# A two-layer encoder: expert weights loaded in 4 KB rows, tokens and results passed through DRAM in slot order

## The chip, the cores and the metric

The kernel runs on one core of a Trainium2 chip. The metric is the device time of one execution in microseconds. Engines are named as in the profile: PE is TensorE (PEld its weight loads), DVE is VectorE, ACT is ScalarE, POOL is GpSimd, SP is SyncE, which here issues the weight loads.

## The reference, cut to what matters

256 tokens of width 1024 pass two layers. Each has a mixer of three branches and a feed-forward part; the second layer's feed-forward part is a mixture of 8 experts of inner width 3584, of which each token takes two:

```python
def swiglu(h, w1, w3, w2):
    return (jax.nn.silu(h @ w1) * (h @ w3)) @ w2

def moe_ffn(h, router, w1, w3, w2):
    logits = (h @ router).astype(jnp.float32)
    top_v, top_i = lax.top_k(logits, TOP_K)
    top_w = jax.nn.softmax(top_v, axis=-1)
    gates = jnp.sum(jax.nn.one_hot(top_i, N_EXPERTS, dtype=jnp.float32) * top_w[..., None], axis=-2)
    ...
    y = gates[..., 0:1] * swiglu(h, w1[0], w3[0], w2[0])
    for e in range(1, N_EXPERTS):
        y = y + gates[..., e:e + 1] * swiglu(h, w1[e], w3[e], w2[e])
    return y
```

All data are float32. The last layer's output is normalized and multiplied by `g_final`.

## The kernel before

**Precision.** A float32 product is made of three products of float32r halves: `mm3` multiplies high by high, high by low and low by high. So each weight tile of 1 MB (a **unit**, 128 partitions x 2048) passes three steps: ACT copies it to its high half `ehi` (`unit_hi`, L830), DVE subtracts to get the low half `elo` in the place of the raw tile (`unit_lo`, L1232), and PE takes 12 matmuls of 512 columns with it (L1397 to L1399).

**Slots.** In the expert stage the tokens of an expert sit in a slot of 128 rows; an expert with more than 128 tokens would get an extra slot of its own. With these inputs there are 8 slots, 0 to 7. Slot 0 is written out, the others are a loop over `s` on each engine (`slot(s)`). A slot has 42 units: per step `f` of 512 inner columns two units each of w1, w3 and w2 (`expert_step`), w2 one step behind the others.

**The path through a slot.** PE writes h@w1 to PSUM `big[0]` and h@w3 to `big[1]`. ACT takes the SiLU into `hid` (L853), DVE multiplies (L1354), PE turns the block with four transposes (L1442; positions `HIDDEN`), ACT and DVE evict it as high and low half (`eahi` L860, `ealo` L1369; positions `TURNED`), and the w2 units use it. After the slot's last unit ACT evicts the result to `ysb` (L841).

**One-hot products.** The tokens of a slot are picked by matrix products: DVE builds the one-hot matrix `Gm` of the next slot, and `gather` (L1718) multiplies `xn` by it in two groups of eight float32 matmuls (16 rows in the trace), after units 38 and 39. Results go back by `spread` (L1727): four float32 matmuls of 512 columns with the turned gate matrix `GT`, after units 4, 6, 8 and 10 of the next slot, each added to `X` by DVE. `GT` is made by two transposes after unit 17. The last slot is spread behind the loop (L1808).

**Buffers.** SP loads units into a ring of 14 (`RING`): the load of unit n waits for PE to be done with unit n-14. `ehi` has three buffers (`EHI`), so ACT's copy of unit n waits for `eunit_done` of unit n-3. Engines run their programs in the order written and meet in semaphores alone; nothing reorders them. GpSimd does little: small loads, and one multiply of `xn` by `g_ffn` (L598) before the stage.

Of the kernel before, what the change touches and what calls it, by code (L numbers as in the profile page):

```python
# [50 lines left out]
FC = 512  # L51
STEPS = FE // FC
UNITS = 6 * STEPS
RING, EHI = 14, 3
# [89 lines left out]
def encoder(nc, ins, out):  # L144
    ctx = ExitStack()
    with ctx:
# [22 lines left out]
        X = keep("X", [P, NB, D])  # L169
        xn = keep("xn", [P, NB, D])  # L170
# [3 lines left out]
        tab = keep("tab", [P, T_W])  # L174
        bmask = keep("bmask", [P, HEADS, SCORE])
        mmask = keep("mmask", [P, SCORE])
        pcol = keep("pcol", [P, ROWS])
# [34 lines left out]
        sd = w("sd", o, [P, 2 * HEADS, SCORE])  # L212
        bhi[2], blo[2] = w("chi", o, [P, 4, TOKENS], F32R), w("clo", o + 4096, [P, 4, TOKENS], F32R)
# [50 lines left out]
        ehi = [w(f"ehi{i}", 8192 * i, [P, 4, 512], F32R) for i in range(EHI)]  # L264
# [3 lines left out]
        at_unit += [8192 * (EHI + i) for i in range(RING - E_GATES - E_MERGED)]  # L268
        assert at_unit[-1] + 8192 <= o
        eraw = [w(f"eraw{i}", a, [P, 4, 512]) for i, a in enumerate(at_unit)]  # L270
        elo = [w(f"elo{i}", a, [P, 4, 512], F32R) for i, a in enumerate(at_unit)]
# [7 lines left out]

        hid = [at(f"hid{i}", over_h + 2048 * i, [SLOT, FC]) for i in range(2)]  # L280
        ahi = [at(f"eahi{i}", over_h + 4096 + 2048 * i, [P, 4, SLOT], F32R) for i in range(2)]
        alo = [at(f"ealo{i}", over_h + 8192 + 2048 * i, [P, 4, SLOT], F32R) for i in range(2)]
        ysb = at("ysb", over_h + 12288, [SLOT, D])
# [25 lines left out]
        gfin = keep("gfin", [P, D])  # L309
        gffn = keep("gffn", [P, D])  # L310

# [88 lines left out]
        g_ready = sem("g_ready")  # L400
        gg_ready = sem("gg_ready")
# [16 lines left out]
        skew_row = HEADS * (2 * TOKENS - 1)  # L418

# [46 lines left out]
        def expert_step(n):  # L466


            if n < 4:
                return 0, n // 2, n % 2  # L470
            if n >= UNITS - 2:
                return STEPS - 1, 2, n % 2
            f, m = (n - 4) // 6 + 1, (n - 4) % 6
            return (f, m // 2, m % 2) if m < 4 else (f - 1, 2, m % 2)


        HIDDEN = [6 * f + 3 if f else 5 for f in range(STEPS)]
        TURNED = [min(6 * f + 5, UNITS - 2) if f else 7 for f in range(STEPS)]
        W1_END = [6 * f - 1 if f else 1 for f in range(STEPS)]
        W3_END = [6 * f + 1 if f else 3 for f in range(STEPS)]  # L480

# [25 lines left out]
        def _(sp):  # L507
# [12 lines left out]
            def expert_unit(e, n):  # L520

                f, m, j = expert_step(n)
                if m < 2:
                    src = ins[("moe_w1", "moe_w3")[m]][0, bass.ds(e, 1), 512 * j:512 * j + 512, FC * f:FC * f + FC]
                else:
                    src = ins["moe_w2"][0, bass.ds(e, 1), FC * f:FC * f + FC, 512 * j:512 * j + 512]
                return src.rearrange("e (k p) n -> p (e k) n", p=P)

            def load_expert(s, e, first=False):
                for n in range(UNITS):  # L530
# [12 lines left out]
                    sp.dma_start(eraw[n % RING][:, :, :], expert_unit(e, n)).then_inc(eraw_in[n % RING], 16)  # L543
# [14 lines left out]
        def _(pool):  # L558
# [27 lines left out]

            pool.wait_ge(x_ready, 8)
# [13 lines left out]


# [4 lines left out]
        EARLY = EHI  # L607
        def gather_bank(s, i):

            return 2 if isinstance(s, int) and s == 0 and i == 1 else 3  # L610
# [6 lines left out]
        def _(act):  # L617
# [219 lines left out]

            def outputs(s):
# [3 lines left out]

            def slot(s, first=False):
                for n in range(UNITS):
                    if not first or n >= EARLY:
# [15 lines left out]
                gathered(s + 1, 1)
# [1003 lines left out]
```

## Time and profile before

| | |
|---|---|
| median of 3 runs | 1719.37 us (1718.28 to 1719.67) |
| the profiled execution | 1720.06 us, of which its span 1718.2 us |
| expert stage, from PE's first unit | about 700 us to 1705 us of the span |
| PE busy | 1676.8 us, 98% |
| weights moved in the expert stage | 336 loads of 1024 KB |

A matmul's end is modelled in the profile, so that neighbours overlap; the time that one takes from its engine is the distance between the starts of two in a row. Where the timeline merges a row (x4), its start is that of the first.

### The profile page before, as it was taken

Reading aid. Unit: us, or ns where it says so; the run is one execution under the profiler, and the core shown is the slowest. Engines: PE = TensorE matmul, PEld = TensorE weight load, DVE = VectorE, ACT = ScalarE, POOL = GpSimd, SP = SyncE. Lnnn points to the kernel's source line nnn. Section 1 sums busy time; section 2 is a strip of 40 time slices with the busy share of each in tenths; the row PEclk is TensorE's granted clock in tenths of the full one; section 3 lists DMA queues with packets and bytes.
Section 4 is the critical chain, followed back from the end, with each engine's and each line's share of the span. In section 5 each row is a group of like instructions: output and inputs, shape, how many; then the busy total and the mean of one; then the engine's idle time right before and its main releaser. Section 6 shows DMA issues by size and latency. Waiting matters only on the chain.

```text
span 1718.2 us, 23329 instructions
## 1 busy us (share of the span) xinstructions
PE 1676.8 (98%) x9215; PEld 1434.6 (83%) x9215; DVE 1269.4 (74%) x991; ACT 1052.6 (61%) x950; POOL 18.7 (1%) x28
## 2 busy tenths in 40 slices
PE   5999999999999999999999999999999999999997
PEld 4899989999889997778788788788788788788786
DVE  4655665544566466898888888898898898888896
ACT  4365645443536454666776776676776777677675
POOL 1000000000000001000000000000000000000000
PEclk8999999999999999999999999999999999999999
DMA  7544454555654448999899999999999999999980
GB/s 236 194 142 145 147 195 148 194 178 176 206 178 142 147 148 318 343 348 376 316 349 374 328 365 354 327 371 344 336 374 339 341 370 338 345 370 339 344 296 25
DMA packets 234687, 468.54 MB, mean 273 GB/s; under 512 B 7553, under 2 KB 11745, under 8 KB 234625
## 3 DMA queue, kind: packets, MB, share of 16 engines
q1 hardware_dynamic: 232400, 459.17, 75.8%
q0 software_dynamic: 1936, 7.44, 1.3%
q8 instruction: 46, 0.75, 0.2%
q10 hardware_dynamic: 288, 1.05, 0.1%
q14 instruction: 17, 0.13, 0.0%
HBM read 465.53 MB, written 2.10 MB: 272 GB/s over the span
## 4 chain that ended last, share of the span: by engine, by line
PE 91%; DVE 4%; ACT 3%; DMA 1%; issue 1%; SPq 0%; DVEq 0%; ACTq 0%
PE big L1397 21%; PE big L1399 21%; PE big L1398 21%; PE small L1397 7%; PE small L1399 7%; PE small L1398 7%; PE small L1442 2%; DVE elo L1232 2%; PE small L1727 1%; ACT ehi L830 1%; PE small L1718 1%; DMA raw<-w_in 1%; ACT whi L628 1%; DVE wlo L906 0%; PE small L1557 0%
## 5 line engine op out<-in xcount | busy, mean ns | idle before, releaser
L1232 DVE TENSOR_TENSOR elo<-eraw,ehi 128x2048 fp32r<-128x2048 f32 x336 | 768.5, 2293 | 106.5 <-ACT ehi L830 105.2
L830 ACT ACTIVATE ehi<-eraw 128x2048 fp32r<-128x2048 f32 x336 | 643.2, 1918 | 180.7 <-PE big L1399 136.8
L906 DVE TENSOR_TENSOR wlo<-raw,whi 128x2048 fp32r<-128x2048 f32 (+2 forms) x104 | 229.9, 2218 | 200.7 <-ACT whi L628 200.7
L1397 PE MATMUL big<-ehi,hehi 128*128 128x512 f32 x896 | 363.6, 406 | 1.4 <-DVE helo L1277 1.4
L628 ACT ACTIVATE whi<-raw 128x2048 fp32r<-128x2048 f32 (+2 forms) x104 | 192.5, 1860 | 264.3 <-PE big L1399 203.5
L1399 PE MATMUL big<-ehi,helo 128*128 128x512 f32 x896 | 350.0, 391 | 0.0
L1398 PE MATMUL big<-elo,hehi 128*128 128x512 f32 x896 | 349.3, 390 | 0.0
L1397 PE MATMUL big<-hhi,whi 128*128 128x256 f32 x864 | 248.1, 287 | 9.8 <-DVE hlo L926 9.8
L1398 PE MATMUL big<-hlo,whi 128*128 128x256 f32 x864 | 245.9, 285 | 0.0
L1399 PE MATMUL big<-hhi,wlo 128*128 128x256 f32 x864 | 245.8, 284 | 0.0
L1397 PEld LDWEIGHTS big<-ehi,hehi 128*128 128x128 f32 x896 | 168.3, 188 | 40.9 <-issue 5.1
L1398 PEld LDWEIGHTS big<-elo,hehi 128*128 128x128 f32 x896 | 168.5, 188 | 38.1 <-issue 5.0
L1399 PEld LDWEIGHTS big<-ehi,helo 128*128 128x128 f32 x896 | 168.1, 188 | 36.4
L1397 PE MATMUL small<-ehi,eahi 128*128 128x512 f32 x448 | 179.8, 401 | 4.0 <-DVE elo L1232 4.0
L1397 PEld LDWEIGHTS big<-hhi,whi 128*128 128x128 f32 x864 | 167.2, 194 | 12.8 <-DVE hlo L926 10.7
L1399 PE MATMUL small<-ehi,ealo 128*128 128x512 f32 x448 | 174.8, 390 | 0.0
L1398 PE MATMUL small<-elo,eahi 128*128 128x512 f32 x448 | 174.6, 390 | 0.0
L1398 PEld LDWEIGHTS big<-hlo,whi 128*128 128x128 f32 x864 | 167.2, 193 | 0.6 <-issue 0.5
L1399 PEld LDWEIGHTS big<-hhi,wlo 128*128 128x128 f32 x864 | 167.2, 194 | 0.0
L1397 PEld LDWEIGHTS small<-ehi,eahi 128*128 128x128 f32 x448 | 84.2, 188 | 27.1 <-DVE elo L1232 6.3
L1398 PEld LDWEIGHTS small<-elo,eahi 128*128 128x128 f32 x448 | 84.2, 188 | 18.2 <-issue 1.7
L1399 PEld LDWEIGHTS small<-ehi,ealo 128*128 128x128 f32 x448 | 84.1, 188 | 17.8
(296 smaller groups left out, 1689.8 us busy)
## 6 DMA issues: line engine op xcount, KB each, us to landing
eraw<-moe_w SPq DMA_DIRECT2D x336, 1024.0 KB, 5.1
raw<-ffn_w SPq DMA_DIRECT2D x30, 1024.0 KB, 5.0
raw<-w_gate SPq DMA_DIRECT2D x24, 1024.0 KB, 5.0
raw<-w_in SPq DMA_DIRECT2D x20, 1024.0 KB, 5.0
raw<-w_branch SPq DMA_DIRECT2D x12, 1024.0 KB, 5.0
raw<-w_o SPq DMA_DIRECT2D x8, 1024.0 KB, 5.0
raw<-w_in SPq DMA_DIRECT2D x4, 896.0 KB, 4.8
raw<-ffn_w SPq DMA_DIRECT2D x6, 512.0 KB, 3.6
```

The costliest lines, as they stand in the source:

```text
L628: act.activation(whi[u % HI][:, 0:kt, 0:cols], raw[u % RAW][:, 0:kt, 0:cols], ACT.Copy).then_inc(hi_ready, 1)
L830: act.activation(ehi[n % EHI][:, :, :], eraw[n % RING][:, :, :], ACT.Copy).then_inc(ehi_ready, 1)
L906: dve.tensor_tensor(wlo[u % RAW][:, 0:kt, 0:cols], raw[u % RAW][:, 0:kt, 0:cols], whi[u % HI][:, 0:kt, 0:cols].bitcast(F32), ALU.subtract) ...
L1232: dve.tensor_tensor(elo[n % RING][:, :, :], eraw[n % RING][:, :, :], ehi[n % EHI][:, :, :].bitcast(F32), ALU.subtract).then_inc(elo_ready, 1)
L1397: pe.matmul(o, sh, mh, start=start, stop=False, **kw)
L1398: pe.matmul(o, sh, ml, start=False, stop=False, **kw)
L1399: return pe.matmul(o, sl, mh, start=False, stop=stop, **kw)
L1442: return pe.transpose(o, src, ident[0:n, 0:n])
L1718: m = pe.matmul(small[:, gather_bank(s, i), SLOT * k:SLOT * k + SLOT], xn[:, b, (4 * i + k) * P:(4 * i + k + 1) * P], Gm[:, b, :], start=b ...
L1727: pe.matmul(small[:, 3, :], GT[:, i // 2, :], ysb[:, half:half + 512], start=True, stop=True).then_inc(spread_done, 1)
```

## The change

**Units.** The inner columns are cut by 1024 (three blocks of 1024, one of 512: `PAIRS`, `pair_width`). A w1 or w3 unit is 256 weight rows of 1024 columns (4 KB in DRAM for each row in place of 2 KB; the last block keeps 512 columns), a w2 unit 256 rows of all 1024 columns. Still 42 units of 1 MB and 12 matmuls each, in the order of `ORDER`. With block p and matrix m (0, 1, 2 for w1, w3, w2) the units are 0-3 (0,0), 4-7 (0,1), 8-11 (1,0), 12-15 (1,1), 16-19 (0,2), 20-23 (2,0), 24-27 (2,1), 28-31 (1,2), 32-33 (3,0), 34-35 (3,1), 36-39 (2,2), 40-41 (3,2). SiLU and multiply take 1024 columns at once; hidden blocks are turned after the units in `TURNS`.

**High halves.** `ehi` has a fourth buffer. Units 0 to 35 go round four buffers, units 36 to 41 round three (`HI_OF`).

**Tokens and results.** GpSimd fills two DRAM tensors with zeros while the dense layer runs, scatters the tokens' rows into `xs_all` in slot order (four indirect transfers in slot 0), and loads a slot's rows for PE, which now turns them with two groups of four transposes, after units 35 and 36 (`GATHERS`). A slot's result is written to `y_all`. In slot 7, four indirect transfers fetch the rows that belong to the tokens, each followed by a multiply and an addition on GpSimd. The last slot is spread by product as before, its `GT` now made behind the loop.

```diff
-FC = 512
-STEPS = FE // FC
-UNITS = 6 * STEPS
-RING, EHI = 14, 3
+ORDER = [(p, m, q) for p, m in ((0, 0), (0, 1), (1, 0), (1, 1), (0, 2), (2, 0), (2, 1), (1, 2), (3, 0), (3, 1), (2, 2), (3, 2))
+         for q in range(pair_units(p))]
+UNITS = len(ORDER)
+TURNS = [9, 10, 18, 19, 30, 31, 37]
+GATHERS = [35, 36]
+RING, EHI, EHI_WORK = 14, 4, 3
+HI_OF = [n % 4 if n < 36 else (n - 36) % 3 for n in range(UNITS)]
...
-        ehi = [w(f"ehi{i}", 8192 * i, [P, 4, 512], F32R) for i in range(EHI)]
+        ehi = [w(f"ehi{i}", 8192 * i, [P, 2048], F32R) for i in range(EHI_WORK)]
+        ehi.append(at("ehi3", over_h, [P, 2048], F32R))
...
+                p, m, q = ORDER[n]
                 if m < 2:
-                    src = ins[("moe_w1", "moe_w3")[m]][0, bass.ds(e, 1), 512 * j:512 * j + 512, FC * f:FC * f + FC]
+                    rows = D // pair_units(p)
+                    src = ins[("moe_w1", "moe_w3")[m]][0, bass.ds(e, 1), rows * q:rows * q + rows,
+                                                       PAIR * p:PAIR * p + pair_width(p)]
-                    src = ins["moe_w2"][0, bass.ds(e, 1), FC * f:FC * f + FC, 512 * j:512 * j + 512]
+                    r = PAIR * p + 256 * q
+                    src = ins["moe_w2"][0, bass.ds(e, 1), r:r + 256, :]
...
+            pool.wait_ge(x_ready, 4)
+            pool.memset(zeros[:, :], 0.0).then_inc(zero_ready, 1)
+            pool.wait_ge(zero_ready, 1)
+            for s in range(SLOTS + 1):
+                pool.dma_start(xs_all[SLOT * s:SLOT * s + SLOT, :], zeros[:, :]).then_inc(zeroed, 16)
+            for s in range(NE - 1, SLOTS):
+                done = y_out if s == NE - 1 else zeroed
+                pool.dma_start(y_all[SLOT * s:SLOT * s + SLOT, :], zeros[:, :]).then_inc(done, 16)
...
+            pool.wait_ge(rows_ready, 1)
+            for c in range(2):
+                for b in range(NB):
+                    pool.indirect_dma_start(xs_all[:, :], bass.IndirectOffsetOnAxis(ap=rowi[:, c, b:b + 1], axis=0),
+                                            xn[:, b, :], None).then_inc(scattered, 16)
+            pool.wait_ge(scattered, 16 * 2 * NB)
+            def slot_in(s):
+                pool.dma_start(xs, xs_all[bass.ds(SLOT * s, SLOT), :]).then_inc(xs_in, 16)
...
+            with pool.Fori(1, last + 1) as s:
+                pool.wait_ge(marked, 2 * s - 1)
+                pool.wait_ge(he_ready, 2 * s + 2)
+                pool.tensor_tensor(mark[:, :], eps[:, :], eps[:, :], ALU.add).then_inc(marked, 1)
+                slot_in(s + 1)
+                pool.wait_ge(marked, 2 * s)
+                pool.wait_ge(y_ready, s)
+                pool.tensor_tensor(mark[:, :], eps[:, :], eps[:, :], ALU.add).then_inc(marked, 1)
+                pool.dma_start(y_all[bass.ds(SLOT * (s - 1), SLOT), :], ysb[:, :]).then_inc(y_out, 16)
+            pool.wait_ge(y_out, 16 * (last + 1))
+            for i in range(2 * NB):
+                pool.indirect_dma_start(ysb[:, :], None, y_all[:, :],
+                                        bass.IndirectOffsetOnAxis(ap=rowi[:, c, b:b + 1], axis=0)).then_inc(early_in, 16)
+                pool.wait_ge(early_in, 16 * (i + 1))
+                pool.tensor_scalar(ysb[:, :], ysb[:, :], gch[:, c, b:b + 1], None, ALU.mult).then_inc(early_scaled, 1)
+                pool.wait_ge(early_scaled, i + 1)
+                pool.tensor_tensor(X[:, b, :], X[:, b, :], ysb[:, :], ALU.add).then_inc(early_added, 1)
...
+                    act.wait_ge(eunit_done, UNITS * s + hi_before(n))
+                act.activation(ehi[HI_OF[n]][:, :], eraw[n % RING][:, :], ACT.Copy).then_inc(ehi_ready, 1)
...
+                        act.wait_ge(y_out, 16 * s)
                         outputs(s - 1)
+                    for p in range(PAIRS):
+                        if n == unit_end(p, 0) + 4:
+                            act.activation(hid[:, 0:pair_width(p)], flat2(big[0][0:SLOT, :, :])[:, 0:pair_width(p)],
+                                           ACT.Silu).then_inc(sil_done, 1)
+                    if n - 4 in GATHERS:
+                        gathered(s + 1, GATHERS.index(n - 4))
+                    if n - 4 in TURNS:
+                        turned(s, t)
...
+            act.wait_ge(early_added, 2 * NB)
             outputs(last)
...
+                if l:
+                    dve.wait_ge(zeroed, 16 * (SLOTS + 1 + SLOTS - NE))
+                    dve.wait_ge(y_out, 16)
...
                     if n == 19 and first:
+                        destinations()
+                    if n == 21 and first:
...
-                    if n == 20:
-                        picked(s + 1)
-                        gated(s + 1)
+                    for p in range(PAIRS):
+                        if n == unit_end(p, 1) + 3:
+                            dve.wait_ge(eunit_done, UNITS * s + unit_end(p, 1) + 1)
+                            dve.wait_ge(sil_done, PAIRS * s + p + 1)
+                            cols = slice(0, pair_width(p))
+                            dve.tensor_tensor(hid[:, cols], hid[:, cols], flat2(big[1][0:SLOT, :, :])[:, cols],
+                                              ALU.mult).then_inc(act_done, 1)
+                    if n - 4 in GATHERS:
+                        gathered(s + 1, GATHERS.index(n - 4))
+                    if n - 4 in TURNS:
+                        turned(s, TURNS.index(n - 4))
...
+            gated(last)
+            dve.wait_ge(gt_done, 1)
...
-            def spread(s, i):
-                pe.matmul(small[:, 3, :], GT[:, i // 2, :], ysb[:, half:half + 512],
-                          start=True, stop=True).then_inc(spread_done, 1)
...
+                    if m == 2:
+                        pe.wait_ge(alo_ready, HE * s + (HE if p == PAIRS - 1 else 2 * p + 1 + q // 2))
...
+                    i.then_inc(eunit_done, 1)
+                    if n in TURNS:
+                        t = TURNS.index(n)
+                        pe.wait_ge(act_done, PAIRS * s + t // 2 + 1)
+                        if t == HE - 1:
+                            pe.wait_ge(he_ready, 2 * s + 3)
                         for k in range(4):
+                            i = turn(small[:, turn_bank(t), SLOT * k:SLOT * k + SLOT], hid[:, c:c + P], SLOT)
+                        i.then_inc(hid_turned, 1)
+                    if n in GATHERS:
+                        j = GATHERS.index(n)
+                        if j == 0:
+                            pe.wait_ge(xs_in, 16 * (s + 1))
+                            pe.wait_ge(alo_ready, HE * s + HE - 1)
...
-                            pe.wait_ge(spread_added, 4 * s)
-                        i.then_inc(gt_done, 1)
-                    if n == UNITS - 4:
-                        pe.wait_ge(gt_ready, s + 1)
-                        gather(s + 1, 0)
-                    if n in HIDDEN:
+                            i = turn(small[:, gather_bank(j), SLOT * k:SLOT * k + SLOT], xs[:, (4 * j + k) * P:(4 * j + k + 1) * P])
...
```

**ACT, the end of a slot** (`REGISTER_ALU` rows carry the waits for the loads). Before, from unit 40's copy (`eraw_149`; unit 41's is `eraw_150`):

```order
L830 ACTIVATE ehi_135<-eraw_149 128x2048 [waits eunit_done]
L834 ISA
L835 ACTIVATE hehi<-small 128x512 [waits gather_done]
L859 REGISTER_ALU
L860 ACTIVATE eahi_172<-small 128x512 [waits hid_turned]
L829 REGISTER_ALU [waits eraw_in13]
L830 ACTIVATE ehi_136<-eraw_150 128x2048 [waits eunit_done]
L834 REGISTER_ALU
L835 ACTIVATE hehi<-small 128x512 [waits gather_done]
```

Now, from unit 39's copy (`eraw_150`) to behind unit 41's (`eraw_152`):

```order
L958 ACTIVATE ehi_135<-eraw_150 128x2048 [waits eunit_done]
L962 ISA
L963 ACTIVATE hehi<-small 128x512 [waits gather_done]
L957 REGISTER_ALU [waits eraw_in12]
L958 ACTIVATE ehi_136<-eraw_151 128x2048 [waits eunit_done]
L962 REGISTER_ALU
L963 ACTIVATE hehi<-small 128x512 [waits gather_done]
L957 REGISTER_ALU [waits eraw_in13]
L958 ACTIVATE ehi_137<-eraw_152 128x2048 [waits eunit_done]
L973 REGISTER_ALU
L975 ACTIVATE last_hi<-small 128x512 [waits hid_turned]
```

Each copy waits until the unit three back is finished, as before: 39's for unit 36, 41's for unit 38. The first gather is evicted behind 39's copy and not behind 40's, the last hidden block (`last_hi`) behind 41's and not ahead of it.

**DVE, the same place.** Before (`elo_163` is unit 40's):

```order
L1232 TENSOR_TENSOR elo_163<-eraw_149,ehi_135 128x2048 [waits ehi_ready]
L1276 ISA
L1277 TENSOR_TENSOR helo<-small,hehi 128x512 [waits hehi_ready]
L1369 TENSOR_TENSOR ealo_174<-small,eahi_172 128x512 [waits ahi_ready]
L1231 REGISTER_ALU
L1232 TENSOR_TENSOR elo_164<-eraw_150,ehi_136 128x2048 [waits ehi_ready]
L1276 REGISTER_ALU
L1277 TENSOR_TENSOR helo<-small,hehi 128x512 [waits hehi_ready]
```

Now (`elo_164` is unit 39's):

```order
L1378 TENSOR_TENSOR elo_164<-eraw_150,ehi_135 128x2048 [waits ehi_ready]
L1422 ISA
L1423 TENSOR_TENSOR helo<-small,hehi 128x512 [waits hehi_ready]
L1377 REGISTER_ALU
L1378 TENSOR_TENSOR elo_165<-eraw_151,ehi_136 128x2048 [waits ehi_ready]
L1422 REGISTER_ALU
L1423 TENSOR_TENSOR helo<-small,hehi 128x512 [waits hehi_ready]
L1377 REGISTER_ALU
L1378 TENSOR_TENSOR elo_166<-eraw_152,ehi_137 128x2048 [waits ehi_ready]
L1500 REGISTER_ALU
L1502 TENSOR_TENSOR last_lo<-small,last_hi 128x512 [waits ahi_ready]
```

The low halves of units 39, 40 and 41 now stand each ahead of one of the three small evictions.

**PE, after unit 37** (the last two matmuls of it, the turn of the last hidden block, and unit 38's first). Now:

```order
L1559 MATMUL small<-elo_162,eahi 128x512
L1560 MATMUL small<-ehi_136,ealo 128x512
L1921 REGISTER_ALU
L1923 REGISTER_ALU [waits act_done]
L1603 MATMUL small<-tab,hid 128x128 [waits he_ready]
L1603 MATMUL small<-tab,hid 128x128 x3
L1902 REGISTER_ALU [waits alo_ready]
L1558 MATMUL small<-ehi_137,eahi 128x512 [waits elo_ready]
```

The turn waits for `he_ready`, the end of the first gather's low half on DVE, since both use the same PSUM bank; units 40 and 41 wait for `alo_ready` of this turn.

**POOL, in slot 7.** None of this was there before:

```order
L724 DMA ysb<-y_all,rowi 128x1024
L727 ISA
L727 TENSOR_SCALAR ysb<-ysb,gch 128x1024 [waits early_in]
L729 TENSOR_TENSOR X<-X,ysb 128x1024 [waits early_scaled]
L724 DMA ysb<-y_all,rowi 128x1024 [waits early_added]
L727 TENSOR_SCALAR ysb<-ysb,gch 128x1024 [waits early_in]
```

The last three rows are the second of four like rounds.

## Rows read from the trace of the kernel before

**Rows 1.** The page, part 1: busy us, share of the span, instructions by engine.
```profile
PE 1676.8 (98%) x9215; PEld 1434.6 (83%) x9215; DVE 1269.4 (74%) x991; ACT 1052.6 (61%) x950; POOL 18.7 (1%) x28
```

**Rows 2.** Windows, one slot: busy of PE, PEld, DVE, ACT, POOL; PEclk, DMA share, GB/s.
```profile
1076.00:1201.80 125.80, 125.53 (x576) 102.49 (x575) 108.55 (x68) 89.03 (x59) 0.00 (x0) 1.00 0.98 351
```

**Rows 3.** Timeline, ScalarE: the eviction of one slot's output and the same six slots later.
```profile
829.89 1.01 ACT L841 ACTIVATE ysb<-small 128x1024 f32<-128x1024 f32 x1
...
1584.47 1.01 ACT L841 ACTIVATE ysb<-small 128x1024 f32<-128x1024 f32 x1
```

**Rows 4.** All waits of TensorE's matmuls in the expert stage.
```profile
PE small L1397 <- DVE elo L1232: 3.7, 11, 0.9
```

**Rows 5.** Timeline, TensorE: one spread product between two units.
```profile
838.75 1.02 PE L1727 MATMUL small<-ysb,GT 128*128 128x512 f32 x2
839.21 0.80 PE L1397 MATMUL big<-ehi,hehi 128*128 128x512 f32 x1
839.85 0.40 PE L1398 MATMUL big<-elo,hehi 128*128 128x512 f32 x1
```

**Rows 6.** Timeline, TensorE: one gather by one-hot products.
```profile
1692.62 1.95 PE L1718 MATMUL small<-Gm,xn 128*128 128x128 f32 x16
1694.33 0.48 PE L1397 MATMUL small<-ehi,eahi 128*128 128x512 f32 x1
1694.64 0.40 PE L1398 MATMUL small<-elo,eahi 128*128 128x512 f32 x1
```

**Rows 7.** Timeline, TensorE: one turn of a hidden block.
```profile
842.38 0.60 PE L1442 MATMUL small<-tab,hid 128*128 128x128 f32 x4
...
843.05 0.40 PE L1398 MATMUL big<-elo,hehi 128*128 128x512 f32 x1
```

**Rows 8.** Groups by line: the high and low halves of a unit.
```profile
L1232 DVE TENSOR_TENSOR elo<-eraw,ehi 128x2048 fp32r<-128x2048 f32 x336 | 768.5, 2293 | 106.5 <-ACT ehi L830 105.2
L830 ACT ACTIVATE ehi<-eraw 128x2048 fp32r<-128x2048 f32 x336 | 643.2, 1918 | 180.7 <-PE big L1399 136.8
```

**Rows 9.** Groups by line in 829.32:957.89: the small evictions.
```profile
L1369 DVE TENSOR_TENSOR ealo<-small,eahi 128x512 fp32r<-128x512 f32 x7 | 4.8, 687 | 3.1 <-ACT eahi L860 3.1
...
L860 ACT ACTIVATE eahi<-small 128x512 fp32r<-128x512 f32 x7 | 4.2, 599 | 11.8 <-PE small L1442 11.8
...
L1277 DVE TENSOR_TENSOR helo<-small,hehi 128x512 fp32r<-128x512 f32 x2 | 1.4, 688 | 0.8 <-ACT hehi L835 0.8
```

**Rows 10.** Timeline: hand-overs between TensorE, ScalarE and VectorE.
```profile
901.49 0.39 PE L1399 MATMUL big<-ehi,helo 128*128 128x512 f32 x1
...
901.92 1.92 ACT L830 ACTIVATE ehi<-eraw 128x2048 fp32r<-128x2048 f32 x1 [0.32 <-PE big L1399]
...
904.64 1.92 ACT L830 ACTIVATE ehi<-eraw 128x2048 fp32r<-128x2048 f32 x1 [0.80 <-PE small L1399]
...
906.59 2.29 DVE L1232 TENSOR_TENSOR elo<-eraw,ehi 128x2048 fp32r<-128x2048 f32 x1 [0.34 <-ACT ehi L830]
```

**Rows 11.** Timeline, TensorE: the wait ahead of a slot's last unit.
```profile
1702.56 0.50 PE L1397 MATMUL small<-ehi,eahi 128*128 128x512 f32 x1 [0.27 <-DVE elo L1232]
```

**Rows 12.** The one GpSimd arithmetic (by source line) and VectorE beside its end (timeline).
```profile
L598 POOL TENSOR_TENSOR xn<-xn,gffn x2: 2355/2370/2385, 682.6 to 684.9; 128x1024 f32<-128x1024 f32 x2
...
686.05 3.42 DVE L1232 TENSOR_TENSOR elo<-eraw,ehi 128x2048 fp32r<-128x2048 f32 x1 [0.76 <-ACT ehi L830]
...
687.26 0.57 POOL L600 DMA_DIRECT2D gfin<-g_final  x1
```

**Rows 13.** Windows: DMA with the queue unheld, and in the dense layer (columns as rows 2).
```profile
670.00:675.00 5.00, 5.00 (x23) 4.13 (x23) 1.28 (x2) 1.34 (x4) 0.00 (x0) 1.00 1.05 408
300.00:400.00 100.00, 100.00 (x707) 94.33 (x706) 48.09 (x24) 40.01 (x24) 0.00 (x0) 1.00 0.57 189
```

**Rows 14.** DMA issues: a 512 KB load from GpSimd, us to landing.
```profile
gffn<-g_ffn POOLq DMA_DIRECT2D x1, 512.0 KB, 7.0
```

**Rows 15.** Timeline, VectorE: one small operation of the routing in slot 0.
```profile
755.59 0.18 DVE L1320 TENSOR_REDUCE gS<-tmp 128x3 f32<-128x24 f32 x1
```

More of the change, by code:

```diff
@@ L169, in encoder @@
         X = keep("X", [P, NB, D])
+        over_xn = place[0]
         xn = keep("xn", [P, NB, D])
@@ L278, in encoder @@
         o += 11264
[L280 to L283, printed above, removed]
+        ysb = at("ysb", over_h + 8192, [SLOT, D])
+        hid = at("hid", over_h + 12288, [SLOT, PAIR])
+        eahi = at("eahi", over_mask, [P, 8, SLOT], F32R)
+        xs = xn[:, 0, :]
+        last_hi = at("last_hi", over_xn + 4096, [P, 4, SLOT], F32R)
+        last_lo = at("last_lo", over_xn + 6144, [P, 4, SLOT], F32R)
         place[0] = work + o
@@ L1758, in slot @@
-                    i.then_inc(eunit_done, 1)
-                    if n in (4, 6, 8, 10) and not first:
-                        if n == 4:
-                            pe.wait_ge(y_ready, s)
-                        spread(s - 1, (n - 4) // 2)
-                    if n == 17:
-                        if not first:
-                            pe.wait_ge(spread_added, 4 * s)
-                        pe.wait_ge(gg_ready, s + 1)
-                        for b in range(NB):
-                            i = turn(small[0:SLOT, 3, b * P:b * P + P], Gg[:, b, :])
-                        i.then_inc(gt_done, 1)
@@ L1788, in slot @@
-                    if n == UNITS - 3:
-                        pe.wait_ge(he_ready, 2 * s + 3)
-                        gather(s + 1, 1)
+                    hi, lo = unit_view(ehi[HI_OF[n]], n), unit_view(elo[n % RING], n)
+                    for k in range(tiles):
+                        t = tiles * q + k
+                        if m < 2:
+                            for half in range(pair_width(p) // 512):
+                                cols = slice(512 * half, 512 * half + 512)
+                                i = mm3(big[m][0:SLOT, half, :], hehi[:, t, :], helo[:, t, :], hi[:, k, cols], lo[:, k, cols],
+                                        t == 0, t == KD - 1)
+                        else:
+                            ahi, alo = hidden_tiles(p)
+                            for half in range(2):
+                                cols = slice(512 * half, 512 * half + 512)
+                                i = mm3(small[0:SLOT, half, :], ahi[:, t, :], alo[:, t, :], hi[:, k, cols], lo[:, k, cols],
+                                        p == 0 and t == 0, n == UNITS - 1 and k == tiles - 1)
@@ L1796, in _ @@
             for i in range(2):
-                gather(0, i)
+                gather(i)
             slot(0, first=True)
@@ L1804, in _ @@
             pe.wait_ge(he_ready, 2 * last + 4)
+            pe.wait_ge(gg_ready, 1)
+            for b in range(NB):
+                i = turn(small[0:SLOT, 2, b * P:b * P + P], Gg[:, b, :])
+            i.then_inc(gt_done, 1)
+            pe.wait_ge(gt_ready, 1)
             pe.wait_ge(y_ready, last + 1)
```

223 lines of the change are left out of this document (127 added, 96 removed).

## The prediction

> **What bounds the kernel now.** I read the page first: PE is busy for 98% of the span [rows 1]. That alone proves little, since neighbouring matmuls overlap in this trace, so I read one slot of the expert stage as a window: PE 125.5 of 125.8 us at full granted clock, DVE 108.6, ACT 89.0, and 351 GB/s of DMA [rows 2]. The period of a slot is (1584.47 - 829.89) / 6 = 125.76 us [rows 3]. Matmuls waited 3.7 us in the whole stage [rows 4]. So PE's own work sets the end of this stage, and a microsecond taken off PE counts, if no wait takes its place.
>
> The period can be rebuilt. From a spread's start to the second matmul behind it are 839.85 - 838.75 = 1.10 us, of which one plain matmul's distance is 0.23: a spread costs 0.87 us, four a slot 3.48 [rows 5]. A gather: 1694.64 - 1692.62 - 0.23 = 1.79, two a slot 3.58 [rows 6]. A turn of a hidden block: 843.05 - 842.38 - 0.23 = 0.44, seven a slot 3.08 [rows 7]. The two turns that make `GT` I put at half of that, 0.2. One wait of 0.27 stands before the last unit [rows 11]. That is 10.6 us; the other 115.2 are 504 matmuls, 0.2285 each, 2.74 us a unit. The change leaves these 504 as they are.
>
> **What comes off PE.** 28 spreads (slots 1 to 7) x 0.87 = 24.4. Of the gathers 16 groups (one pair is made in each slot for the next) become turns of the same form as a hidden block's: 16 x (1.79 - 0.44) = 21.6. `GT` is made once in place of 8 times: 7 x 0.2 = 1.4; the one left lies at the end beside ACT's eviction of `ysb` (1.0 us [rows 3]). The old waits go: 8 x 0.27 = 2.2. Sum 49.6 us.
>
> **What new waits take.** The order now ties PE's late turns to DVE and ACT, so I follow the end of a slot. A copy on ACT starts 0.20 us after the last matmul of the unit that it waits for has had its time (901.49 + 0.23 to 901.92), lasts 1.92, and DVE starts 0.03 later (904.64 + 1.92 to 906.59) [rows 10]; the low half lasts 2.29 [rows 8], a small low half 0.69 [rows 9], and PE starts some 0.06 behind DVE.
>
> First wait: PE's turn after unit 37 waits for the first gather's low half (`he_ready`). DVE makes it behind the low half of unit 39, whose copy waits for unit 36. From the end of unit 36: 0.20 + 1.92 + 0.03 + 2.29 + 0.69 + 0.06 = 5.19 us. PE meanwhile has the second gather's turn and unit 37: 0.44 + 2.74 = 3.18. It waits 2.0.
>
> Second wait: unit 40 needs the low half of the last hidden block. DVE makes it behind the low half of unit 41, whose copy waits for unit 38. Again 5.19 us from the end of unit 38 (ACT's eviction, 0.60, lies beside DVE's 2.29 [rows 9]), and PE has only unit 39, 2.74. It waits 2.45. Both waits come in each of 8 slots: 35.6 us. The rest of the chains have room: other turns stand three units or more ahead of their users, SiLU and multiply of 1024 columns (about 1.0 and twice 0.7) come off PE's path by two units, and four `ehi` buffers give DVE a lead of 3 x 2.74 - 4.5 = 3.7 us where three gave 1.0. The lower bound of this term is nothing (if I misread the order), the upper 45, if ACT is late once more for each slot.
>
> **GpSimd in slot 7.** Eight arithmetic instructions of 128x1024, and the only row of that kind is 2.36 us [rows 12]. The same rows show the danger: the second ran from 684.9 to 687.26, DVE's `elo` began at 686.05 and took 3.42 us in place of 2.29. It lost 1.13 of the 1.2 us in which both ran, so it stood still. If all eight hold up DVE, 8 x 2.36 = 18.9 us go. DVE is busy for most of its time (42 x 2.29 + about 10.5 of small work = 107 of the slot's 123 us), but the lead of 3.7 absorbs the first round, and in each of three pauses (a fetch of 512 KB landed in 7.0 us [rows 14], with its issue perhaps 9) it wins back 3.5 x (2.74 - 2.29) = 1.6. So 18.9 - 3.7 - 4.8 = 10 us late. Bounds: 0 and 18.9. The rounds start early in slot 7 and take about 4 x (9 + 4.7) = 55 us, so they end before the slot does.
>
> The Trainium skill's page "SBUF — State Buffer", section "Who interferes with whom", says that a DVE instruction with two SBUF inputs and a GpSimd instruction that reads SBUF exclude each other for a whole instruction. By that rule all eight count, as in the row; the page adds nothing to the size.
>
> **What is hidden.** Slot 0 gets 16 more small DVE operations of about 0.2 us [rows 15], 3.3 us against a lead of 3.7; the three waits of this kind that are there now (about 1.5 us in the 3.7 of [rows 4]) stay as large. The zeros are 16 transfers of 512 KB, 8 MB, in the dense layer, where DMA moves 189 GB/s and could move 408 [rows 13]: some 40 us of spare rate, and weights are loaded there four units ahead; uncovered it would be 2 to 5 us. The scatter and the first load have from unit 19 to unit 35, 44 us. Writing a result needs `ysb` free one slot later.
>
> **DMA.** A slot now moves 42 x 1.05 + 2 x 0.52 = 45.1 MB. In 123.7 us that is 365 GB/s against 351. With nothing holding the queue back, rows of 2 KB already came at 408 GB/s [rows 13]. So the longer rows buy nothing, and the rate is there.
>
> A rule speaks against this. The Trainium skill's page "DMA: Bandwidth & Descriptors", section "Specifications", gives about 358 GB/s as the limit of HBM for a core; by it a slot would take 45.1 / 358 = 126 us and nothing would be won. The trace has more than that rate, so the row decides.
>
> **The sum.** 49.6 - 35.6 - 10 = 4.0 us less: 1716.1 against the profiled execution's 1720.06. The median of the runs shown is 0.7 lower, so 1715.4. Within 0.2% (3.4 us, about what a measurement of this kernel can tell) means 1716.0 to 1722.8; I stand just past its edge. A slot's period goes from 125.76 to 125.76 - 3.48 - 3.58 - 0.2 - 0.27 + 0.88 + 4.45 = 123.6.
>
> **The rivals.**
> - *GpSimd costs nothing on the path* (its operations shorter, or DVE not stopped): 14.0 us less, 1705.4. For it: the overlap was seen once, over 1.2 us. Chance 0.2.
> - *GpSimd costs more, and the kernel is slower*: same place, slot 7. Against what was saved up to then (14.0), it decides from a loss of 14.0 + 3.4 = 17.4 us on. With the same cover of 8.5 that is (17.4 + 8.5) / 8 = 3.2 us for one operation, a third above the row; at 4 us the loss is 23.5 and the time 1728.9. For it: a multiply by a column's scalar has no row, and DVE in turn holds up GpSimd. Chance 0.2.
> - *The two late waits are not there or half there* (PE finds its turn ready): up to 35.6 less, 1680 to 1698. Against it: the same chain, one small eviction shorter, gives the 0.27 us of [rows 11]. Chance 0.1.
> - *DMA becomes the bound*, at the 351 GB/s at which it runs now: 45.1 / 351 = 128.5 us a slot, 7 x 2.7 = 19 us more, about 1740. Against it rows 13. Chance 0.05.
> - Another wait that I don't see, or zeros and scatter uncovered: 1720 to 1728. Chance 0.05.
>
> My forecast, 1711 to 1721 around 1715.4, has 0.4, of which half lies past 0.2%. The range reaches to the first two rivals: 1699 to 1729. Faster: 0.2 + 0.2 + 0.1, less what of the free case falls short, 0.47; same 0.2 and the mild part of dear GpSimd, 0.26; slower 0.27.
>
> **What would show it.** In the profile after: no spread inside the loop and eight transposes of `xn` a slot on PE; a slot's period of 123.6; PE waiting 2.0 us for DVE `helo` and 2.5 us for DVE `last_lo` (before unit 40) in every slot; `elo` instructions of up to 4.6 us beside eight GpSimd operations in slot 7, whose length is about 10 us above the others. The forecast is wrong if those waits are absent, if GpSimd's operations are far from 2.36 us, or if waits on `eraw_in` appear on ACT.

## The result, and the profile after

The median of four runs is 1703.13 us (1702.68 to 1703.97) against 1718.82 us before (1718.27 to 1719.67, four runs on the same chip); the ratio is 0.9908, 95% interval [0.9895, 0.9922]. The profiled execution took 1703.97 us, its span 1702.1. The forecast was 1715.4, so the change gave 15.7 us where 4 were expected. That is inside the whole range (1699 to 1729), outside the likeliest case (1711 to 1721), and close to the time of the rival in which GpSimd costs nothing (1705.4).

The page, part 1, of the changed kernel:

```profile
PE 1632.4 (96%) x8953; PEld 1403.5 (82%) x8953; DVE 1249.7 (73%) x916; ACT 1046.9 (62%) x926; POOL 101.7 (6%) x92
```

PE is busy for 44.4 us less than in [rows 1], and the span is only 16 us shorter. The rest is waiting. All waits of PE between 700 and 1690 us of the changed kernel:

```profile
PE small L1558 <- DVE last_lo L1502: 18.3, 8, 2.3
PE small L1603 <- DVE helo L1423: 14.1, 8, 1.9
PE big L1558 <- DVE helo L1423: 1.4, 1, 1.4
```

The first two are the forecast's two late waits, once in each slot and of nearly the forecast size; the third stands at the head of the stage in both kernels. The waits of [rows 4] are gone. Windows, one slot (columns as in [rows 2]), and timeline, ScalarE's eviction of the output of slots 0, 3, 6 and 7:

```profile
1200.60:1323.73 123.13, 119.10 (x542) 97.98 (x541) 104.66 (x56) 88.28 (x58) 2.95 (x4) 1.00 0.98 366
```

```profile
829.56 1.01 ACT L969 ACTIVATE ysb<-small 128x1024 f32<-128x1024 f32 x1
...
1200.60 1.00 ACT L969 ACTIVATE ysb<-small 128x1024 f32<-128x1024 f32 x1
...
1569.99 1.00 ACT L969 ACTIVATE ysb<-small 128x1024 f32<-128x1024 f32 x1
...
1689.44 1.02 ACT L969 ACTIVATE ysb<-small 128x1024 f32<-128x1024 f32 x1 [8.36 <-PE small L1560]
```

(1569.99 - 1200.60) / 3 = 123.13 us a slot, against 125.76 in [rows 3] and 123.6 forecast. The last slot holds GpSimd's work and should have been 10 us longer. From its wait before the turn behind unit 37 to that of the slot before are 1673.11 - 1549.97 = 123.14 us (the starts of the last matmul ahead of each wait): it isn't longer at all. The GpSimd operations are there, as the timeline of GpSimd shows for two of the four rounds:

```profile
1588.70 3.62 POOL L727 TENSOR_SCALAR ysb<-ysb,gch 128x1024 f32<-128x1024 f32 x1 [6.09 <-DMA ysb<-y_all,rowi]
1592.40 2.79 POOL L729 TENSOR_TENSOR X<-X,ysb 128x1024 f32<-128x1024 f32 x1
...
1603.88 6.11 POOL L727 TENSOR_SCALAR ysb<-ysb,gch 128x1024 f32<-128x1024 f32 x1 [5.64 <-DMA ysb<-y_all,rowi]
1610.07 2.58 POOL L729 TENSOR_TENSOR X<-X,ysb 128x1024 f32<-128x1024 f32 x1
```

And VectorE's low halves beside the four rounds, those that took longer than the 2.28 us of their neighbours (timeline), and all of this stretch (groups by line in 1580:1690: busy us, mean ns):

```profile
1592.84 4.50 DVE L1378 TENSOR_TENSOR elo<-eraw,ehi 128x2048 fp32r<-128x2048 f32 x1
...
1607.31 3.08 DVE L1378 TENSOR_TENSOR elo<-eraw,ehi 128x2048 fp32r<-128x2048 f32 x1
1610.31 4.50 DVE L1378 TENSOR_TENSOR elo<-eraw,ehi 128x2048 fp32r<-128x2048 f32 x1
...
1625.27 2.60 DVE L1378 TENSOR_TENSOR elo<-eraw,ehi 128x2048 fp32r<-128x2048 f32 x1
1628.39 3.89 DVE L1378 TENSOR_TENSOR elo<-eraw,ehi 128x2048 fp32r<-128x2048 f32 x1
...
1643.63 2.71 DVE L1378 TENSOR_TENSOR elo<-eraw,ehi 128x2048 fp32r<-128x2048 f32 x1 [0.34 <-ACT ehi L958]
1647.39 3.37 DVE L1378 TENSOR_TENSOR elo<-eraw,ehi 128x2048 fp32r<-128x2048 f32 x1
...
L1378 DVE TENSOR_TENSOR elo<-eraw,ehi 128x2048 fp32r<-128x2048 f32 x35 | 87.4, 2530 | 7.9 <-ACT ehi L958 7.8
```

Beyond 2.28 us each, VectorE lost 2.2, 3.0, 1.9 and 1.5 us in the four rounds, 8.7 together, which agrees with 35 x (2.53 - 2.28). The rounds come some 18 us apart, and each loss is smaller than the lead of 3.7 us. What is left of the lead is seen where PE takes a unit, at its tightest for the low half that began at 1615.86 (timelines of DVE and PE):

```profile
1615.86 2.28 DVE L1378 TENSOR_TENSOR elo<-eraw,ehi 128x2048 fp32r<-128x2048 f32 x1
...
1619.11 0.48 PE L1558 MATMUL small<-ehi,eahi 128*128 128x512 f32 x1
```

1619.11 - 1615.86 - 2.28 = 1.0 us; for the same unit of the slot before it is 3.5.

One thing was not foreseen. In slots 0 and 2 PE ran at half its clock behind a late wait. Timeline of PE, slot 2:

```profile
1066.37 0.49 PE L1558 MATMUL small<-ehi,last_hi 128*128 128x512 f32 x1 [2.29 <-DVE last_lo L1502]
1066.69 0.39 PE L1559 MATMUL small<-elo,last_hi 128*128 128x512 f32 x1
...
1068.42 0.63 PE L1559 MATMUL small<-elo,last_hi 128*128 128x512 f32 x1
1068.85 0.63 PE L1560 MATMUL small<-ehi,last_lo 128*128 128x512 f32 x1
...
1071.50 0.40 PE L1558 MATMUL small<-ehi,last_hi 128*128 128x512 f32 x1
1071.73 0.40 PE L1559 MATMUL small<-elo,last_hi 128*128 128x512 f32 x1
```

Starts are 0.43 us apart instead of 0.23. The window over this place has the granted clock (third column from the right) at 0.52, the lower of the two levels, 1.2 in place of 2.4 GHz:

```profile
1067.50:1071.00 3.50, 3.50 (x11) 2.70 (x10) 0.93 (x1) 0.20 (x1) 0.00 (x0) 0.52 0.59 242
```

Just before, PE had stood idle for 1.74 us (until 1057.93) and 2.29 us (until 1066.37). The slot with this stretch took 1077.46 - 952.69 = 124.77 us, 1.64 more than its neighbours.

### The profile page after: what moved, and what is told of

It is laid out like the page before. It is cut to its first block, busy times and chain, and to the rows that moved or that the text cites. A ratio compares the mean times of both kernels' runs of the same rounds, so it can differ in the third digit from the quotient of the medians.

```text
span 1702.1 us, 22766 instructions
## 1 busy us (share of the span) xinstructions
PE 1632.4 (96%) x8953; PEld 1403.5 (82%) x8953; DVE 1249.7 (73%) x916; ACT 1046.9 (62%) x926; POOL 101.7 (6%) x92
## 4 chain that ended last, share of the span: by engine, by line
PE 89%; ACT 4%; DVE 3%; issue 2%; DMA 2%; SPq 0%; DVEq 0%; ACTq 0%
PE big L1558 21%; PE big L1560 21%; PE big L1559 21%; PE small L1558 6%; PE small L1560 6%; PE small L1559 6%; PE small L1603 2%; ACT ehi L958 2%; DMA raw<-ffn_w 1%; DMA raw<-w_in 1%; ACT whi L756 1%; DVE elo L1378 0%; DVE wlo L1049 0%; PE small L1718 0%; PE small L1658 0%
## 5 line engine op out<-in xcount | busy, mean ns | idle before, releaser
L1558 PE MATMUL big<-ehi,hehi 128*128 128x512 f32 x896 | 352.0, 393 | 1.4 <-DVE helo L1423 1.4
L1558 PE MATMUL small<-ehi,eahi 128*128 128x512 f32 x384 | 153.5, 400 | 0.0
L1560 PE MATMUL small<-ehi,ealo 128*128 128x512 f32 x384 | 150.1, 391 | 0.0
L1559 PE MATMUL small<-elo,eahi 128*128 128x512 f32 x384 | 149.6, 390 | 0.0
L1560 PEld LDWEIGHTS small<-ehi,ealo 128*128 128x128 f32 x384 | 72.1, 188 | 15.8
L1559 PEld LDWEIGHTS small<-elo,eahi 128*128 128x128 f32 x384 | 72.3, 188 | 14.0
L1558 PEld LDWEIGHTS small<-ehi,eahi 128*128 128x128 f32 x384 | 72.2, 188 | 13.7
```

Of the source, the lines that this page charges most:

```text
L1558: pe.matmul(o, sh, mh, start=start, stop=False, **kw)
L1559: pe.matmul(o, sh, ml, start=False, stop=False, **kw)
L1560: return pe.matmul(o, sl, mh, start=False, stop=stop, **kw)
```

## The experiments

Their times are medians with the ratio to the kernel before, whose median was 1719.18 us beside x1 to x4 and 1719.90 beside x5 to x8. For small differences I also give the **stage time**, from PE's first expert matmul to the last eviction of `ysb`, since PE begins the stage anywhere between 698.4 and 700.5 us, whatever is changed in it. Before it is 1705.61 - 699.70 = 1005.91 us, after 1689.44 - 700.24 = 989.20. A stage time is that of one execution, the profiled one: of its kernel's runs it took the least time for x2 and x4, the most for after, x3, x6 and x8.

### x1: the late units get their high buffers earlier

The theory was that the two late waits come from ACT's copies, which in the last six units wait for the unit three before.

```diff
-HI_OF = [n % 4 if n < 36 else (n - 36) % 3 for n in range(UNITS)]
+HI_OF = [n % 4 if n < 24 else 1 + (n - 24) % 3 if n < 30 else (n - 30) % 4 for n in range(UNITS)]
```

> Edit: the six units that go round three high buffers stand at units 24 to 29 in place of the slot's end, so that the copies of units 39 and 41 wait for units 35 and 37. Nothing else changes. Theory (the two late waits cost what they last): from unit 35 on the first chain takes 5.2 us against 6.4 of PE's work, the second 5.2 against 5.9, so both waits vanish: 32.4 us of waits and about 3 us at the lower clock behind two of them go, period 123.1 to about 119.0, time about 1667. Rival 1 (DMA is the bound behind them): 45.1 MB in 119 us would be 379 GB/s; if it can't be had, ACT waits for loads and the time stays above 1680. Rival 2 (VectorE is the bound behind them): waits for the low half appear at units 24 to 29 or in slot 7, time 1675 or more.

Measured: 1665.28 us (1664.23 to 1666.03), ratio 0.9686 [0.967, 0.9702]. PE's waits in the stage:

```profile
PE big L1558 <- DVE helo L1423: 1.4, 1, 1.4
PE small L1558 <- DVE elo L1378: 1.0, 1, 1.0
```

Both late waits are gone. In their place stands one wait of 1.0 us in slot 7: the order now has three high buffers, and so a lead of only 1.0 us, in units 24 to 29, and GpSimd's last addition holds up the low half of one of them (1605.40 to 1609.80, PE starts at 1609.85). PE and the DMA in nearly one slot (windows), and the loads of the weights (DMA issues, KB each, us to landing):

```profile
1060.00:1170.00 110.00, 110.00 (x504) 91.01 (x503) 97.31 (x53) 81.40 (x53) 2.02 (x4) 1.00 1.01 379
```

```profile
eraw<-moe_w SPq DMA_DIRECT2D x336, 1024.0 KB, 6.2
```

In this slot PE never stops, at full clock. The stage time is 1650.70 - 699.83 = 950.87, 38.3 less than after: 32.4 - 1.0 of waits, 3.3 of half clock, 16 x 0.09 = 1.4 for PE's restarts (1066.69 - 1066.37 = 0.32 us to the next start in place of 0.23), and most of the last 2.2 is what the list of waits leaves out: it counts from the modelled end of the matmul ahead, 0.39 us behind its start, where the next could have begun 0.23 behind it, 15 x 0.16 = 2.4. A slot takes 118.6 us and its 45.1 MB run at 380 GB/s, so DMA was not the bound at 366. The Trainium skill's page "DMA: Bandwidth & Descriptors", section "Specifications", has about 358 GB/s as HBM's limit for a core; this trace goes past it for the length of the stage.

### x2: GpSimd only fetches

Each round keeps the indirect fetch. The scaling and the addition to `X` are replaced with an addition of one column, so this kernel leaves the results of slots 0 to 6 out of its output.

```diff
-                pool.tensor_scalar(ysb[:, :], ysb[:, :], gch[:, c, b:b + 1], None, ALU.mult).then_inc(early_scaled, 1)
-                pool.wait_ge(early_scaled, i + 1)
-                pool.tensor_tensor(X[:, b, :], X[:, b, :], ysb[:, :], ALU.add).then_inc(early_added, 1)
+                pool.tensor_tensor(shift[:, i:i + 1], eps[:, :], eps[:, :], ALU.add).then_inc(early_added, 1)
```

> Edit: the four fetches in slot 7 stay, the multiply and the addition behind each are left out (one addition of 128x1 in their place), so the results of slots 0 to 6 are not added to the output. Theory (the lead of the four high buffers hides them): no change, within 1 us of the changed kernel's 1703.1. Rival (they cost on the path as predicted, 10 us, and something else won them back): 1693.

Measured: 1704.16 us (1700.52 to 1705.59), ratio 0.9916 [0.9899, 0.9932], no less than with the arithmetic. PE's waits are unchanged (18.3 and 14.1 us). The stage time is 1685.97 - 698.35 = 987.62, 1.6 below after; this execution has one stretch at half clock (at 943 us) where after has two. So GpSimd's eight operations cost the changed kernel nothing that these runs can tell (the medians differ by 1.0 us, the runs of x2 among themselves by 5).

### x3: rows of 2 KB again

A unit is loaded by two transfers of half its columns, 512 KB each.

```diff
-                    sp.dma_start(unit_view(eraw[n % RING], n), expert_unit(e, n)).then_inc(eraw_in[n % RING], 16)
+                    dst, src = unit_view(eraw[n % RING], n), expert_unit(e, n)
+                    sp.dma_start(dst[:, :, 0:dst.shape[2] // 2], src[:, :, 0:dst.shape[2] // 2]).then_inc(eraw_in[n % RING], 16)
+                    sp.dma_start(dst[:, :, dst.shape[2] // 2:], src[:, :, dst.shape[2] // 2:]).then_inc(eraw_in[n % RING], 16)
```

> Edit: each expert unit is loaded by two transfers of half its columns, so that a row in DRAM is 2 KB (1 KB for w1 and w3 of the last block) in place of 4 KB; all else as in the changed kernel. Theory (the longer rows buy nothing while PE is the bound): same time, 1703 within 2 us, landing of a unit a little later. Rival (the longer rows are needed for 366 GB/s): waits of ACT for loads, 1715 or more.

Measured: 1703.61 us (1701.86 to 1704.65), ratio 0.9906 [0.989, 0.9923]. The loads (x672) landed in 6.0 us and PE's waits were the same. The longer rows by themselves bought nothing, as forecast.

### x4: the spreads back on PE

```diff
+                    if n in (4, 5, 6, 8) and not first:
+                        pe.matmul(small[:, 3, :], ident, tab[:, 0:512], start=True, stop=True)
```

> Edit: in slots 1 to 7 four float32 matmuls of 512 columns (the form of the old spread, of the identity by a constant table, into an unread bank) are issued after units 4, 5, 6 and 8. Theory (a spread costs PE 0.87 us each and nothing hides it): 28 x 0.87 = 24.4 us more, 1727.5. Rival (PE has room elsewhere, the spreads were cheap): under 12 us more.

Measured: 1731.71 us (1730.24 to 1732.51), ratio 1.0075 [1.0058, 1.0092], 28.6 above after and slower than before. One such product on PE's timeline:

```profile
840.26 1.02 PE L1919 MATMUL small<-tab 128*128 128x512 f32 x2
840.72 0.80 PE L1558 MATMUL big<-ehi,hehi 128*128 128x512 f32 x1
841.36 0.40 PE L1559 MATMUL big<-elo,hehi 128*128 128x512 f32 x1
```

841.36 - 840.26 - 0.23 = 0.87 us, as in [rows 5]. The stage time is 1715.68 - 699.58 = 1016.10, 26.9 above after: 28 x 0.87 = 24.4, one stretch at half clock more (1.6), and 0.9 over. The forecast's price of a spread stands.

### x5: PE kept awake in the late waits

```diff
+            def filler(count):
+                for _ in range(count):
+                    pe.matmul(big[0][:, 1, 0:256], ident, tab[:, 0:256], start=True, stop=True)
```

`filler(3)` stands ahead of the wait before the turn behind unit 37, `filler(4)` ahead of unit 40.

> The changed kernel with seven matmuls of 256 columns whose result nobody reads: three ahead of the wait before the turn behind unit 37, four ahead of unit 40, so that TensorE does something while it waits. Theory: the 0.43 us spacing of about eight matmuls behind the late waits of slots 0 and 2 is the clock gone down to 1.2 GHz because TensorE stood idle just before; with the fillers both stretches keep the full granted clock, the fillers lie inside the waits of 1.9 and 2.3 us and cost nothing, and about 2 x 1.6 us go: 1700. Rival: the clock falls there for another reason; then both stretches stay and the time is 1703 or, if the fillers reach past the waits, up to 1 us per slot more, 1711.

Measured: 1699.55 us (1698.76 to 1701.28), ratio 0.9885 [0.9869, 0.9902]. Both fillers fit into the waits:

```profile
PE small L1558 <- DVE last_lo L1502: 4.5, 8, 0.6
PE small L1603 <- DVE helo L1423: 3.6, 8, 0.5
```

No window of the stage is below full clock. Windows over the two places:

```profile
818.00:822.00 4.00, 4.00 (x19) 3.31 (x18) 1.14 (x2) 1.92 (x1) 0.00 (x0) 1.00 0.82 279
...
1066.00:1071.00 5.00, 5.00 (x24) 4.14 (x23) 2.37 (x2) 3.94 (x3) 0.00 (x0) 1.00 0.82 275
```

The stage time is 1684.59 - 698.71 = 985.88, 3.3 below after, twice 1.64. Nothing that the kernel computes with comes sooner, so it is PE's idling that lowers the clock. The other traces agree: the stage has no stretch at half clock in the kernels without these waits (before, x1), and 1 to 5 in each of the six that have them unfilled (after, x2, x3, x4, x6, x7).

### x6: five GpSimd operations in a row

```diff
+                for k in range(2):
+                    pool.wait_ge(early_scaled, 4 * i + k + 1)
+                    pool.tensor_tensor(ysb[:, :], ysb[:, :], ysb[:, :], ALU.add).then_inc(early_scaled, 1)
+                pool.wait_ge(early_scaled, 4 * i + 3)
+                pool.tensor_scalar(ysb[:, :], ysb[:, :], 0.25, None, ALU.mult).then_inc(early_scaled, 1)
```

> The changed kernel with three more whole-tile GpSimd instructions (two additions of ysb to itself, one multiplication by 0.25) behind each scaling, so 20 in place of 8, five in a row. Theory 'each GpSimd instruction stops VectorE for its whole length': VectorE loses 20 x 2.36 = 47 us, less the lead of 3.7 us and the 0.45 us that it wins back on each of some 40 units meanwhile (18): 25 us more, 1728. Rival 'GpSimd mostly waits for VectorE': the trace of the changed kernel has 7 us lost in four pieces for 8 instructions, 0.9 each; then 20 cost VectorE 18 us, about what it wins back: 1703 to 1706. A burst of five that costs one low half each (about 1.1 to 2.2 us) would give 5 x 1.6 = 8 us a round, 4 more than lead and recovery carry in the first, and lie between: about 1712.

Measured: 1713.3 us (1709.28 to 1719.46), ratio 0.9957 [0.9943, 0.9971]: between the theories, at the middle value. The profiled execution took the most of the five (1719.46). Two of GpSimd's additions in its third round, and the low halves beside them (timelines):

```profile
1647.76 2.07 POOL L730 TENSOR_TENSOR ysb<-ysb 128x1024 f32<-128x1024 f32 x1
1649.91 3.82 POOL L730 TENSOR_TENSOR ysb<-ysb 128x1024 f32<-128x1024 f32 x1
...
1648.00 3.98 DVE L1383 TENSOR_TENSOR elo<-eraw,ehi 128x2048 fp32r<-128x2048 f32 x1
1651.90 3.98 DVE L1383 TENSOR_TENSOR elo<-eraw,ehi 128x2048 fp32r<-128x2048 f32 x1
```

The two engines take turns. The low half ahead of these ended at 1648.07. The first addition ends 1.76 us later (1649.83), the first low half 2.15 later (1651.98), the second addition 1.75 later (1653.73), the second low half 2.15 later (1655.88). So neither instruction works while the other does, and each row's length holds its wait for the other. It is so in all ten traces: each of the 58 low halves that an addition of GpSimd held up, the one of [rows 12] among them, ends 2.15 us behind the end of that addition (within 0.01). A scaling lets go earlier: each of the 31 low halves that one held up ends 0.40 us behind it, so that it began its work 1.75 us before the scaling's end. The Trainium skill's page "SBUF — State Buffer", section "Who interferes with whom", lets such instructions exclude each other entirely. These traces agree for the additions, and for a scaling up to its last 1.75 us.

A held instruction therefore costs VectorE what is left of the other when its own turn has come: 1.70 us for an addition to `ysb` (3.98 - 2.28), at most 2.2 for one to `X`, at most 0.9 for a scaling. Low halves of slot 7 in x6 (groups by line, as for the changed kernel):

```profile
L1383 DVE TENSOR_TENSOR elo<-eraw,ehi 128x2048 fp32r<-128x2048 f32 x35 | 101.9, 2957 | 1.0 <-ACT ehi L963 0.9
```

VectorE lost 35 x (2.957 - 2.28) = 23.7 us, 1.2 for each of 20 operations; after it is 8.7, 1.1 for each of 8. The lead and what VectorE wins back cover the smaller sum and not the larger. PE's waits at the end of x6 (1600 to 1700 us):

```profile
PE small L1608 <- DVE helo L1428: 5.0, 1, 5.0
PE big L1563 <- DVE elo L1383: 3.0, 4, 1.4
PE small L1563 <- DVE last_lo L1507: 2.3, 1, 2.3
PE small L1563 <- DVE elo L1383: 1.2, 2, 0.8
```

4.2 us are new, and the wait before the last turn is 5.0 in place of 1.7. The clock falls behind it:

```profile
1685.00:1690.00 5.00, 2.81 (x9) 2.42 (x10) 4.94 (x4) 0.00 (x0) 0.00 (x0) 0.50 0.00 0
```

### x7: three high buffers in the whole slot

```diff
-HI_OF = [n % 4 if n < 36 else (n - 36) % 3 for n in range(UNITS)]
+HI_OF = [n % 3 for n in range(UNITS)]
...
-RING, EHI, EHI_WORK = 14, 4, 3
+RING, EHI, EHI_WORK = 14, 3, 3
```

> The changed kernel with three buffers for the high halves all through (unit n in buffer n modulo 3) in place of four up to unit 35 and three behind. Theory: the fourth buffer is VectorE's lead, 3.7 us against 1.0. The late waits have three buffers in both and stay 1.9 and 2.3 us. Without the lead a turn at the head of a slot comes about 0.3 us late once a slot (2.5 us in all), and the four low halves that GpSimd stretches by 2.2, 2.2, 1.6 and 1.1 us each reach past 1.0 us: 3.1 us. Sum 1708.7. Rival: the lead does nothing in this order, 1703.

Measured: 1715.95 us (1712.93 to 1719.02), ratio 0.9977 [0.9966, 0.9989]: 12.8 above after, where 5.6 were expected. Without the fourth buffer four fifths of the change's gain are gone. PE's waits in slot 0, and in the last slot:

```profile
PE big L1558 <- DVE elo L1378: 3.4, 4, 1.3
PE small L1558 <- DVE last_lo L1502: 2.3, 1, 2.3
PE small L1603 <- DVE helo L1423: 1.9, 1, 1.9
```

```profile
PE small L1603 <- DVE hid L1523: 2.1, 1, 2.1
PE big L1558 <- DVE elo L1378: 1.9, 3, 1.0
```

I had left out slot 0: there the fourth buffer hides VectorE's small routing work, 3.4 us. GpSimd's work in the last slot costs 4.0 (3.1 expected), the six slots between 0.24 each (0.3 expected). The rest is the clock. The windows show five stretches at half clock, two in slot 0 and one each in slots 2, 6 and 7, three more than after, 4.9 us. The stage time rose by 1004.81 - 989.20 = 15.6; 3.4 + 4.0 + 1.4 + 4.9 = 13.7 of it are named, 1.9 in slot 0 are not.

### x8: x1 with x6's twenty operations

> The kernel with the buffers of the late units rearranged (1665.3) and the same twenty GpSimd instructions in its last slot. TensorE waits nowhere else there, so what VectorE loses past its lead shows undiluted, and a slot is 4.6 us shorter, so VectorE wins back less (its 105 us of work in 118.5 instead of 123.1). Whole-length theory: 25 to 30 us more, 1692. Mostly-waiting theory: 0 to 3 us more, 1665 to 1668. Between: about 1675.

Measured: 1676.91 us (1676.38 to 1677.74), ratio 0.975 [0.9734, 0.9767], 11.6 above x1: the middle value again. PE's waits from 1500 to 1662 us:

```profile
PE small L1608 <- DVE helo L1428: 4.8, 1, 4.8
PE small L1563 <- DVE elo L1383: 2.3, 3, 1.0
PE big L1563 <- DVE elo L1383: 1.4, 1, 1.4
```

8.5 us against 1.0 in x1, and about 2.2 at half clock behind the first. So GpSimd's price is not hidden by the late waits that x1 removed: it is nothing until VectorE's lead is used up.

## Why the prediction was off, step by step

- **What bounds the kernel.** Right. PE's own work and its waits set the stage in every run.
- **What comes off PE.** Right. The spread's 0.87 us came back in x4, and a gather turn in the trace after takes 1050.30 - 1049.63 - 0.23 = 0.44 us, as put. Only the old waits were too small: I expected 1.5 of the 3.7 us of [rows 4] to stay in slot 0, and none did. The fourth buffer covers slot 0's small operations too, as x7 shows.
- **The new waits.** Right in place, cause and number. The turn waited 14.1 / 8 = 1.76 us where 2.0 were put, unit 40 waited 2.29 where 2.45 were: 32.4 in place of 35.6. x1 shows the cause, since another order of the same buffers removes both.
- **GpSimd in slot 7: the step that failed.** "18.9 - 3.7 - 4.8 = 10 us late" measured 0 (x2; the last slot's length). The failed term is the 18.9. [rows 12] were read rightly: the low half stood still, and it did so beside every addition. But the price is not the 2.36 us of the GpSimd instruction. GpSimd first waits for the low half under way (its scalings lasted 3.6 to 7.1 us), and only the next low half is held up: 2.2, 2.2, 1.6 and 1.1 us by the four additions, 0, 0.8, 0.3 and 0.4 by the scalings, 8.7 in all. The cover was right: with the forecast's own 3.7 and 4.8 this gives 8.7 - 8.5 = 0.2. It held in each round too, with 1.0 us of the lead left at the tightest place. x6 and x8 give the other end: with 23.7 us lost in x6, PE is late.
- **What I did not have: the clock.** Two stretches of 3.5 us at half clock behind the late waits cost 3.3 us (x5).
- **DMA and the rows of 4 KB.** Right: x3 shows that the rows buy nothing, and x1 that 380 GB/s are there.
- **The sum.** Over the stage: 49.6 + 1.5 - 32.4 - 3.3 - 0 = 15.4, against 16.7 measured; 1.3 stay unplaced (PE's restarts and the 0.16 us that the list leaves out of each wait, 16 waits now and 11 before, would add 1.3 to that). PE began the stage 0.5 us later after (700.24 against 699.70), so the profiled execution gained 16.1.
- **The likeliest case** (1711 to 1721) was wrong. The first rival has the right time, but not for its reasons: GpSimd's operations took 2.6 us and more, and VectorE was stopped by them; what it lost was small enough for its lead and the pauses. That the time comes within 2.3 us of that rival's is partly luck, since smaller late waits (3.2) and the old waits (1.5) about cancel the clock (3.3).

The version that beats both kernels is x1, 1665.3 us.

## What to carry to other kernels

Where two engines take turns, ask what is left of the other's instruction when your own could begin, not how long that instruction is. Compare a disturbance with the lead piece by piece: pieces smaller than the lead and far enough apart to be won back cost nothing, and the same work in one burst costs its excess. Where buffers are cut down at the end of a loop body to make the wrap come out, follow that end by hand and look for another rotation before taking a wait for given; here one line of buffer numbers was worth 38 us, more than twice the whole change. A wait of 2 us on TensorE may cost more than its length, so look at the granted clock behind it.

## What the runs showed of the hardware

- Waits of 1.7 and 2.3 us, about 8 us apart, were now and then followed by a stretch of about 3.5 us at 1.2 GHz, worth 1.6 us. Which slots it hits changes between executions and kernels: slots 0 and 2 after, slot 1 alone in x2. Idle matmuls in the waits prevent it (x5). In x2 the mean granted clock was 0.996 in the run of 1700.52 us and 0.992 in that of 1705.59, so this is probably part of why its runs differ by 5 us and those of x1 and x5 by 1.8 and 2.5; only one run of each has a trace.
- VectorE's low half (two inputs in SBUF) and a GpSimd addition exclude each other: the one that is under way ends first, then the other works. A held-up low half ends 2.15 us behind the addition (58 of 58), an addition to `X` 2.27 us behind the low half that it waited for (1595.19 - 1592.92).
- A scaling of 128x1024 on GpSimd (one input and a column) took 2.85 us where it had not to wait (x6, at 1617.11), and holds VectorE's low half up only until 1.75 us before its end (31 of 31).
- A slot's 45.1 MB came at 380 GB/s, slot after slot (x1), and the landing time of a 1 MB load only rose from 5.4 to 6.2 us.
